# Prompt attention: the two maps of a differential head joined into one P row

## The chip, the cores and the metric

The kernel runs on one core of one Trainium2 chip. The metric is the device time of one execution in microseconds. Matmuls run on TensorE (PE; its weight loads are PEld), row arithmetic on VectorE (DVE), exponentials and copies out of PSUM on ScalarE (ACT); GpSimd (POOL) and the DMA queues are the others. Engines run their own instruction lists in order and meet only at semaphores.

## The reference, cut to what matters

One layer of a hybrid encoder over a prompt of 2048 tokens with 16 leading meta tokens (2064 rows), and over eight sampled streams. The stage in question is attention over the prompt:

```python
# group A: 8 heads of 64; each query attends to its top 256 admissible keys
_, sel = lax.top_k(score, k_top)
p = jax.nn.softmax(logits, axis=-1)
o = einsum('bqhk,bqkd->bqhd', p, v_sel)
# group B: 4 differential heads, two maps c each, values of 128
logits = einsum('bqhcd,blhcd->bhcql', qb, kb) * DH_B ** -0.5
logits = where(adm, logits - slope * dist, -inf)
p = softmax(logits, axis=-1)
a = p[:, :, 0] - lam * p[:, :, 1]
o = einsum('bhql,blhe->bqhe', a, vb)
```

After it come an RMS norm over each head of B, the output projection and an MLP.

## The kernel before, in words

The kernel is five stages with a barrier after each: keys' projection, queries' projection with the index scores, attention of the samples, attention of the prompt (`attend_prompt`), and the feed-forward stage. Only `attend_prompt` matters here.

It walks over 16 tiles `t` of 128 queries. Tile `t` sees `n = 16 + 128 (t + 1)` keys. In each tile there are 16 jobs `g % JOBS = m`: m = 0 to 7 are the heads of A, m = 8 to 15 are the eight maps of B, two by two. One job is, in order:

- PE: the logits of 128 queries by `n` keys, in pieces ("halves") of 1024 columns into one of two buffers `LG` (line 1098). They are computed two jobs ahead, inside the apply of an earlier job.
- VectorE, `take` (line 1270): adds the distances (`DT`, or `DA` for heads of A, where the keys that are not selected are far away), writes the row `X`, and keeps the maximum `mx`; line 1276 multiplies the maximum by the slope (`nm`).
- ScalarE, `softmax` (line 1179): the exponential in place, with its sum `sm`.
- PE, `apply`: transposes of `X` in groups of four 128-blocks into two banks `TP` (line 1125), ScalarE's copy of each group to `PTr` (line 1202), products of `PTr` with the values into `PV` (line 1138).
- VectorE: reciprocal of the sum (line 1284), and the output: line 1303 for A; for B line 1306 puts the first map's result into `OM`, and line 1311 adds the second's, multiplied by minus lambda over its sum (`rl`, line 1291).

There are two rows `X`, so the mask pass of job g + 1 waits for the transposes of job g - 1 (`s_tr`).

Beside the jobs VectorE finds for tile t + 1 each query's 256th largest index score: 25 halvings, each a count over the row. VectorE counts every other one (line 825, between the small steps 830 and 834), ScalarE the rest by signs (line 1187, `count_signs`). Nine last steps (lines 838 to 854, one of them a scan, line 846) make the row `DA`. The function `select_steps(m)` gives the steps of each job: halvings in jobs 2 to 14, the last steps in jobs 14 and 15, in front of the mask pass of the next tile's first job.

At a tile's end `finish` takes the norms of the four B heads, GpSimd raises them to the power -0.5 (lines 1066 and 1069), `finish_scale` applies them, and PE and ScalarE transpose the tile's output at job 2 of the next tile. SyncE's queue loads keys, values, queries and scores and stores the transposed output.

## Time and profile before

| | |
|---|---|
| median of 3 runs | 4177.35 us (4172.96 to 4182.59) |
| the profiled execution | 4171.43 us, span 4169.9 us |
| PE busy, whole span | 3748.4 us (90%) |
| VectorE busy | 2326.8 us (56%) |
| ScalarE busy | 1676.0 us (40%) |
| GpSimd busy | 186.8 us (4%) |
| prompt attention | about 995 to 2376 us of the span |
| PE, VectorE, ScalarE busy in it | 1181, 1068, 920 us |
| granted TensorE clock in it | 0.92 of full speed |

How to read it: an engine's busy time is a sum over the whole stage, but the tiles differ: early ones are short and full of small instructions, late ones long and full of matrix work, and the last has no selection beside it. So the stage is read tile by tile and job by job. The chain of work that ended last lies wholly in the feed-forward stage, behind the barrier, and says nothing about this stage.

### The profile page before, as it was taken

Reading aid. Unit: us, or ns where it says so; the run is one execution under the profiler, and the core shown is the slowest. Engines: PE = TensorE matmul, PEld = TensorE weight load, DVE = VectorE, ACT = ScalarE, POOL = GpSimd, SP = SyncE. Lnnn points to the kernel's source line nnn. Section 1 sums busy time; section 2 is a strip of 40 time slices with the busy share of each in tenths; the row PEclk is TensorE's granted clock in tenths of the full one; section 3 lists DMA queues with packets and bytes.
Section 4 is the critical chain, followed back from the end, with each engine's and each line's share of the span. In section 5 each row is a group of like instructions: output and inputs, shape, how many; then the busy total and the mean of one; then the engine's idle time right before and its main releaser. Section 6 shows DMA issues by size and latency. Waiting matters only on the chain. (4 is left out here: it accounts for less than half of the span.)

```text
span 4169.9 us, 56226 instructions
## 1 busy us (share of the span) xinstructions
PE 3748.4 (90%) x20713; PEld 3178.6 (76%) x20713; DVE 2326.8 (56%) x4784; ACT 1676.0 (40%) x2562; POOL 186.8 (4%) x373
## 2 busy tenths in 40 slices
PE   8989996884788988888988799999999999989997
PEld 6877883443677878888987678877888788779996
DVE  4335651444788888888775344445445444544334
ACT  2223431112566767777875422232323232322221
POOL 0001110000000000000000010001000100010000
PEclk9999995996799999999999899999999999999998
DMA  5556435627322121111100132223223322322121
GB/s 156 156 153 207 158 131 170 201 69 194 74 50 55 40 51 35 35 36 37 26 16 16 52 131 86 105 101 131 101 101 111 111 102 99 126 96 80 61 79 46
DMA packets 279876, 394.51 MB, mean 95 GB/s; under 512 B 29584, under 2 KB 181136, under 8 KB 270864
## 3 DMA queue, kind: packets, MB, share of 16 engines
q1 hardware_dynamic: 244208, 336.77, 25.9%
q0 software_dynamic: 12160, 44.18, 3.3%
q10 hardware_dynamic: 23328, 11.22, 1.1%
q8 instruction: 106, 1.74, 0.2%
q14 instruction: 74, 0.61, 0.0%
HBM read 320.32 MB, written 71.80 MB: 94 GB/s over the span
## 5 line engine op out<-in xcount | busy, mean ns | idle before, releaser
L1138 PE MATMUL pPV<-pV,pPTr 128*128 128x128 f32 (+1 forms) x4864 | 651.4, 282 | 36.8 <-ACT pPTr L1202 21.4
L1138 PEld LDWEIGHTS pPV<-pV,pPTr 128*128 128x128 f32 x4864 | 613.8, 198 | 57.6 <-issue 15.7
L1202 ACT ACTIVATE pPTr<-pTP 128x512 f32<-128x512 f32 (+3 forms) x704 | 355.7, 535 | 284.2 <-PE pTP L1125 281.5
L2167 ACT ACTIVATE fRU<-fUP 128x512 f32<-128x512 f32 (+1 forms) x128 | 80.0, 625 | 930.6 <-PE fUP L2037 930.6
L2037 PE MATMUL fUP<-fA_hi,fW_hi 128*128 128x512 f32 (+1 forms) x1280 | 418.9, 360 | 20.0 <-DVE fA_lo L2209 20.0
L2037 PE MATMUL fDN<-fW_hi,fU_hi 128*128 128x512 f32 x1088 | 423.6, 389 | 2.1 <-DVE fY L2307 2.1
L2037 PE MATMUL fDN<-fW_lo,fU_hi 128*128 128x512 f32 x1088 | 423.4, 389 | 0.0
L2037 PE MATMUL fDN<-fW_hi,fU_lo 128*128 128x512 f32 x1088 | 423.2, 389 | 0.0
L2037 PE MATMUL fUP<-fA_lo,fW_hi 128*128 128x512 f32 (+1 forms) x1280 | 418.3, 359 | 0.0
L2037 PE MATMUL fUP<-fA_hi,fW_lo 128*128 128x512 f32 (+1 forms) x1280 | 417.8, 359 | 0.0
L2203 DVE TENSOR_TENSOR fW_lo<-fW_raw,fW_hi 128x2048 fp32r<-128x2048 f32 x144 | 333.3, 2336 | 129.6 <-ACT fW_hi L2122 129.6
L1125 PE MATMUL pTP<-pidn,pX 128*128 128x128 f32 x2432 | 363.5, 281 | 35.0 <-ACT pX L1179 28.1
L1179 ACT ACTIVATE pX<-pX,pnm 128x144 f32<-128x144 f32 (+15 forms) x256 | 311.1, 1215 | 125.2 <-DVE pnm L1276 125.1
L2307 DVE TENSOR_TENSOR fY<-fDN,fY 128x512 f32<-128x512 f32 x272 | 183.6, 690 | 283.7 <-PE fDN L2037 283.7
L1125 PEld LDWEIGHTS pTP<-pidn,pX 128*128 128x128 f32 x2432 | 296.4, 152 | 39.7 <-ACT pX L1179 29.3
L1098 PE MATMUL pLG<-pK,pQA 128*128 128x512 f32 (+4 forms) x704 | 186.8, 399 | 138.2 <-DVE pmx L1270 103.5
L2122 ACT ACTIVATE fW_hi<-fW_raw 128x2048 fp32r<-128x2048 f32 x144 | 270.1, 1901 | 26.7 <-DMA fW_raw<-w_o 21.6
L2282 DVE TENSOR_TENSOR fU<-fRU 128x512 f32<-128x512 f32 (+1 forms) x128 | 92.9, 725 | 336.4 <-ACT fRU L2167 336.4
L2037 PEld LDWEIGHTS fUP<-fA_hi,fW_hi 128*128 128x128 f32 x1280 | 232.0, 189 | 51.8 <-issue 21.1
L1098 PEld LDWEIGHTS pLG<-pK,pQA 128*128 128x128 f32 x704 | 136.5, 212 | 165.8 <-DVE pmx L1270 92.5
L825 DVE TENSOR_SCALAR_CACHE_REDUCE pjunk<-pS,psv 128x272 int8<-128x272 f32 (+14 forms) x180 | 257.3, 1430 | 6.4
L2037 PEld LDWEIGHTS fUP<-fA_hi,fW_lo 128*128 128x128 f32 x1280 | 231.7, 189 | 30.6
(237 smaller groups left out, 6254.2 us busy)
## 6 DMA issues: line engine op xcount, KB each, us to landing
fW_raw<-w_up SPq DMA_DIRECT2D x64, 1024.0 KB, 5.0
fW_raw<-w_down SPq DMA_DIRECT2D x64, 1024.0 KB, 4.9
qT<-qOUT SPq DMA_DIRECT2D x40, 512.0 KB, 3.3
sKB<-cache_kb SPq DMA_DIRECT2D x8, 2048.0 KB, 14.0
sVB<-cache_vb SPq DMA_DIRECT2D x8, 2048.0 KB, 8.4
pQA<-qT SPq DMA_DIRECT2D x64, 256.0 KB, 4.9
pQB<-qT SPq DMA_DIRECT2D x64, 256.0 KB, 5.0
fW_raw<-w_o SPq DMA_DIRECT2D x16, 1024.0 KB, 5.5
```

The source lines that it names most:

```text
L825: ins = dve.tensor_scalar(junk, S, mid, 0.0, ALU.is_ge, ALU.add, accum_out=cnt)
L1098: mm = pe.matmul(dst[:, b - a:b - a + size], q[:, u, :], K[:, km, b:b + size], start=(u == 0), stop=(u == 1))
L1125: tr = pe.transpose(bank[:, j - 4 * k, :], X[g % 2][:, j * P:(j + 1) * P], idn[:, :])
L1138: mm = pe.matmul(PV[g % 2][:, 0:size], PTr[n % 3][:, j - 4 * k, :], V[:, j, a:a + size], start=(j == 0), stop=(j == blk[t] - 1))
L1179: act.activation(X[g % 2][:, 0:n_of[t]], X[g % 2][:, 0:n_of[t]], ACT.Exp, bias=nm[:, g % 2:g % 2 + 1], scale=slope, accum_out=sm[:, g % 2: ...
L1202: act.activation(PTr[n % 3][:, 0:size, :], TP[bank_use[("p", n)] % 2][:, 0:size, :], ACT.Copy).then_inc(s_pt, 1)
L2037: mm = pe.matmul(o, stationary[a], m[b], start=first and i == 0, stop=last and i == 2)
L2122: act.activation(W_hi[j // 2][:, (j % 2) * 2048:(j % 2) * 2048 + 2048], W_raw[j % 2][:, :], ACT.Copy).then_inc(s_whi, 1)
L2167: act.activation(RU[:, 0:nt * P].rearrange("p (n w) -> p n w", n=n), UP[f % 2][:, 0:n, 0:width], ACT.Relu).then_inc(s_ru, 1)
L2203: dve.tensor_tensor(W_lo[j // 2][:, col], W_raw[j % 2][:, :], W_hi[j // 2][:, col].bitcast(F32), ALU.subtract).then_inc(s_wlo, 1)
L2282: dve.tensor_tensor(U2[:, 0:nt * P], RU[:, 0:nt * P], RU[:, 0:nt * P], ALU.mult).then_inc(s_u2, 1)
L2307: dve.tensor_tensor(Y[:, t, cols], DN[o % 4][:, :], Y[:, t, cols], ALU.add)\
```

## The change

For a differential head with unnormalised rows e1, e2 and sums s1, s2 the result is (e1/s1 - lam e2/s2) V. The new kernel forms the row e1 + c e2 with c = -lam s1/s2, transposes and multiplies that one row, and scales the output by 1/s1.

- `applied(g)`: only the odd maps of B have an apply. An even map's place in PE's order holds its logits-ahead alone.
- `combine` on VectorE: the coefficient `cf`, then one pass over the first three quarters of the columns (`cut(t)`). GpSimd joins the last quarter in two passes, a product and a sum. The apply waits for both (`s_cb`, `s_pa`).
- There are three rows `X` (`XB`), and logits, mask pass and exponential run one job further ahead (`AHEAD = 3`; `take(g + 2)`, `softmax(g + 2)`).
- The mask pass takes the slope itself (scale `-SLOPE[m]`, minimum in place of maximum), and `nm` with its instruction goes.
- Reciprocals are taken for two jobs at once (`invert_sums`), at even jobs; `OM` and `rl` leave the outputs.
- Inside an apply only the first piece of the coming logits stands early, the others before the last group of products (before: the first two early).
- The selection starts and ends a job earlier: sign counts in jobs 0 to 12, the nine last steps in job 13. It stands last in VectorE's job, and no longer has outputs and reciprocals between its small steps.
- `lam4` lies in `OT`.

```diff
+    XB, AHEAD = 3, 3
+    def applied(g):
+        return g % JOBS < H_A or g % 2 == 1
...
-        X = [sb(f"X{i}", [P, XW]) for i in range(2)]
+        X = [sb(f"X{i}", [P, XW]) for i in range(XB)]
...
+        def cut(t):
+            return n_of[t] // 32 * 24
...
         def counted_by_sign(m):
-            return 2 * (m - 1) if 0 <= 2 * (m - 1) < HALVINGS else None
+            return 2 * m if 2 * m < HALVINGS else None
         def select_steps(m):
+            last = HALVINGS // 2
             if m == 0:
+                return 0, 1
+            if m <= last:
+                return count(2 * m - 2) + 1, count(2 * m)
+            if m == last + 1:
+                return count(2 * m - 2) + 1, SEL
+            return SEL, SEL
...
+            def combine(g):                      # GpSimd
+                t = g // JOBS
+                j = combined_before(g)
+                part = slice(cut(t), n_of[t])
+                x = X[(g + 1) % XB][:, part]
+                c = cf[:, j % 2:j % 2 + 1].to_broadcast([P, n_of[t] - cut(t)])
+                pool.wait_ge(s_cf, j + 1)
+                pool.tensor_tensor(x, x, c, ALU.mult).then_inc(s_pm, 1)
+                pool.wait_ge(s_pm, j + 1)
+                pool.tensor_tensor(x, x, X[g % XB][:, part], ALU.add).then_inc(s_pa, 1)
...
             def apply(g):                        # PE
                 if m < H_A:
+                    pe.wait_ge(s_ex, g + 1)
                 else:
+                    pe.wait_ge(s_cb, combined_before(g))
+                    pe.wait_ge(s_pa, combined_before(g))
...
-                        queries_keys(g + 2, slice(0, 2))
+                        logits(g + AHEAD, slice(0, 1))
                     products(k - 1)
-                if g + 2 < NG:
-                    queries_keys(g + 2, slice(2, None) if early else slice(None))
+                if g + AHEAD < NG:
+                    logits(g + AHEAD, slice(1, None) if early else slice(None))
                 products(groups[t] - 1)
...
             for g in range(NG):
-                apply(g)
+                if applied(g):
+                    apply(g)
+                elif g + AHEAD < NG:
+                    logits(g + AHEAD)
...
+            def invert_sums(g):                  # VectorE
+                i = g % 4
+                dve.wait_ge(s_ex, g + 2)
+                if g >= 4:
+                    dve.wait_ge(s_out, outputs_before(g - 2))
+                dve.reciprocal(ri[:, i:i + 2], sm[:, i:i + 2]).then_inc(s_ri, 1)
+            def combine(g):
+                dve.wait_ge(s_ri, g // 2 + 1)
+                if j >= 2:
+                    dve.wait_ge(s_pm, j - 1)
+                dve.tensor_scalar(c, sm[:, i:i + 1], lv[:, 5:6], ri[:, i + 1:i + 2], ALU.mult, ALU.mult)\
+                    .then_inc(s_cf, 1)
+                dve.wait_ge(s_cf, j + 1)
+                x = X[(g + 1) % XB][:, 0:n]
+                dve.scalar_tensor_tensor(x, x, c, X[g % XB][:, 0:n], ALU.mult, ALU.add).then_inc(s_cb, 1)
...
             take(0)
+            take(1)
             for g in range(NG):
+                if g + 2 < NG:
+                    take(g + 2)
+                if m % 2 == 0:
+                    invert_sums(g)
+                    if m >= H_A:
+                        combine(g)
+                if g > 0 and applied(g - 1):
+                    output(g - 1)
                 if m == 0 and t > 0:
                     finish(t - 1)
+                if t + 1 < PT:
+                    for k in range(*select_steps(m)):
+                        select(t + 1, k)
                 if m == 0 and t > 0:
                     finish_scale(t - 1)
```

## Rows read from the trace of the kernel before

**Rows 1.** Windows: the stage, then tiles 3, 9, 13 and 15; busy us per engine.

```profile
995.00:2376.00 1381.00, 1181.38 (x8827) 1107.13 (x8828) 1068.04 (x3131) 920.23 (x1636) 19.24 (x32) 0.92 0.20 47
...
1153.00:1210.00 57.00, 46.42 (x315) 43.32 (x315) 47.12 (x183) 35.93 (x93) 1.49 (x4) 0.86 0.25 55
...
1569.00:1661.00 92.00, 81.09 (x634) 77.34 (x632) 78.68 (x215) 67.20 (x109) 1.31 (x3) 0.94 0.17 39
...
1987.00:2108.00 121.00, 107.92 (x857) 102.83 (x856) 97.49 (x215) 87.61 (x125) 1.20 (x2) 0.94 0.11 23
...
2241.00:2373.00 132.00, 122.24 (x949) 113.01 (x947) 50.92 (x146) 69.62 (x110) 1.23 (x3) 1.00 0.02 5
```

**Rows 2.** Waits inside the stage: total us, times, longest.

```profile
DVE pX L1270 <- PE pTP L1125: 163.4, 91, 6.0
...
PE pLG L1098 <- DVE pmx L1270: 107.1, 27, 14.9
```

**Rows 3.** Timeline of VectorE at the end of tile 13: start, us.

```profile
2079.53 2.23 DVE L840 TENSOR_SCALAR_CACHE_REDUCE pDA<-pS,psv 128x1936 f32<-128x1936 f32 x1
...
2096.60 1.22 DVE L1270 CUSTOM_DVE_ANT_0 pX<-pLG,pDA 128x1024 f32<-128x1024 f32 x1
```

**Rows 4.** Timeline of one job B of tile 13, PE and VectorE.

```profile
2056.29 1.22 DVE L1270 CUSTOM_DVE_ANT_0 pX<-pLG,pDT 128x1024 f32<-128x1024 f32 x1 [0.43 <-PE pTP L1125]
...
2058.45 1.88 PE L1098 MATMUL pLG<-pK,pQB 128*128 128x512 f32 x8
...
2058.75 0.15 DVE L1276 TENSOR_SCALAR pnm<-pmx 128x1 f32<-128x1 f32 x1
...
2059.38 2.23 DVE L825 TENSOR_SCALAR_CACHE_REDUCE pjunk<-pS,psv 128x1936 int8<-128x1936 f32 x1
...
2060.16 1.05 PE L1138 MATMUL pPV<-pV,pPTr 128*128 128x128 f32 x8
...
2062.91 1.23 DVE L1270 CUSTOM_DVE_ANT_0 pX<-pLG,pDT 128x1024 f32<-128x1024 f32 x1 [0.72 <-PE pTP L1125]
```

**Rows 5.** Costliest groups: ScalarE's copies of transposed blocks.

```profile
L1202 ACT ACTIVATE pPTr<-pTP 128x512 f32<-128x512 f32 (+3 forms) x704 | 355.7, 535 | 284.2 <-PE pTP L1125 281.5
```

**Rows 6.** VectorE passes with two row operands: ns min/median/max over the 15 tiles.

```profile
L844 DVE SCALAR_TENSOR_TENSOR pDA<-pS,psv,pDA x15: 502/1434/2369, 1035.7 to 2210.3; 128x272 f32<-128x272 f32 x1, 128x400 f32<-128x400 f32 x1, 128x528 f32<-128x528 f32 x1, 128x656 f32<-128x656 f32 x1
```

**Rows 7.** Feed-forward stage: GpSimd's add alone, then one among VectorE's subtracts.

```profile
2430.30 1.89 POOL L2011 TENSOR_TENSOR fY<-fconst 128x1024 f32<-128x1024 f32 x1 [28.24 <-ACT fY L2145]
...
2445.70 2.21 POOL L2011 TENSOR_TENSOR fY<-fconst 128x1024 f32<-128x1024 f32 x1 [13.51 <-ACT fY L2145]
...
L2203 DVE TENSOR_TENSOR fW_lo<-fW_raw,fW_hi x2: 2280/3131/3982, 2446.1 to 2450.0; 128x2048 fp32r<-128x2048 f32 x2
```

**Rows 8.** Timeline: outputs of jobs 7, 15 of tile 9; last copies, tile 13.

```profile
1607.65 0.28 DVE L1303 TENSOR_SCALAR pO<-pPV,pri 128x64 f32<-128x64 f32 x1
...
1659.12 0.35 DVE L1311 SCALAR_TENSOR_TENSOR pO<-pPV,prl,pOM 128x128 f32<-128x128 f32 x1
...
2036.45 0.49 ACT L1202 ACTIVATE pPTr<-pTP 128x384 f32<-128x384 f32 x1 [0.58 <-PE pTP L1125]
...
2103.93 0.49 ACT L1202 ACTIVATE pPTr<-pTP 128x384 f32<-128x384 f32 x1 [0.62 <-PE pTP L1125]
```

**Rows 9.** Timeline of VectorE in tile 15: the mask passes of two jobs B.

```profile
2339.02 1.22 DVE L1270 CUSTOM_DVE_ANT_0 pX<-pLG,pDT 128x1024 f32<-128x1024 f32 x1 [4.51 <-PE pTP L1125]
...
2347.56 1.23 DVE L1270 CUSTOM_DVE_ANT_0 pX<-pLG,pDT 128x1024 f32<-128x1024 f32 x1 [4.66 <-PE pTP L1125]
```

**Rows 10.** Windows of PE alone in tiles 1 and 2: busy, granted clock.

```profile
1061.00:1064.00 3.00, 2.76 (x12) 0.50 0.58 175
...
1098.00:1100.00 2.00, 0.00 (x0) 1.00 0.18 33
...
1102.00:1104.00 2.00, 2.00 (x11) 0.50 0.00 0
...
1110.00:1112.00 2.00, 1.89 (x12) 0.70 0.50 154
```

More of the change, by code:

```diff
@@ L869, in attend_prompt @@
     NG = PT * JOBS
+    SLOPE = SLOPE_A + [s for s in SLOPE_B for _ in range(2)]
+    def applied(g):
+        return g % JOBS < H_A or g % 2 == 1
     sems = []
@@ L944, in groups_before, with outputs_before, combined_before @@
         def groups_before(g):
-            return sum(groups[i // JOBS] for i in range(g))
+            return sum(groups[i // JOBS] for i in range(g) if applied(i))
+        def outputs_before(g):
+            return sum(1 for i in range(g) if applied(i))
+        def combined_before(g):
+            return sum(1 for i in range(g) if not applied(i))
         def bank_users():
-            logits, banks, use_of, bank_use = [], [], {}, {}
-            def logit(kind, n, free):
-                use_of[kind, n] = len(logits)
-                logits.append(free)
+            banks, bank_use = [], {}
             def bank(kind, n, free):
@@ L1063, in _ @@
             pool.wait_ge(s_half, 1)
-            for t in range(PT):
-                pool.wait_ge(s_fq, 4 * (t + 1))
-                pool.tensor_scalar(fs[:, 4:8], fs[:, 0:4], 1.0 / DV_B, EPS, ALU.mult, ALU.add)\
-                    .then_inc(s_fe, 1)
-                pool.wait_ge(s_fe, t + 1)
-                pool.tensor_tensor(fs[:, 4:8], fs[:, 4:8], half[:, :], ALU.pow).then_inc(s_fr, 1)
+            def combine(g):
[8 more added lines that the diff above has]
+                pool.tensor_tensor(x, x, X[g % XB][:, part], ALU.add).then_inc(s_pa, 1)
+            for t in range(PT + 1):
+                if t > 0:
+                    pool.wait_ge(s_fq, 4 * t)
+                    pool.tensor_scalar(fs[:, 4:8], fs[:, 0:4], 1.0 / DV_B, EPS, ALU.mult, ALU.add)\
+                        .then_inc(s_fe, 1)
+                    pool.wait_ge(s_fe, t)
+                    pool.tensor_tensor(fs[:, 4:8], fs[:, 4:8], half[:, :], ALU.pow).then_inc(s_fr, 1)
+                if t < PT:
+                    for m in range(H_A, JOBS, 2):
+                        combine(t * JOBS + m)
         @block.tensor
@@ L1089, in free_bank, with logits @@
                 return TP[u % 2]
[L1091 to L1102 removed]
+            def logits(g, some=slice(None)):
                 t, m = divmod(g, JOBS)
@@ L1162, in finish @@
                     tr.then_inc(s_ft, 1)
-            queries_keys(0)
-            queries_keys(1)
+            for g in range(AHEAD):
+                logits(g)
             for g in range(NG):
@@ L1193, in take @@
                 t = g // JOBS
-                for k in range(groups[t]):
-                    if k == 2 and g + 1 < NG:
-                        softmax(g + 1)
+                for k in range(groups[t] if applied(g) else 0):
+                    if k == 2 and g + 2 < NG:
+                        softmax(g + 2)
                     n = groups_before(g) + k
@@ L1203, in take @@
                                    ACT.Copy).then_inc(s_pt, 1)
-                if groups[t] <= 2 and g + 1 < NG:
-                    softmax(g + 1)
+                if (groups[t] <= 2 or not applied(g)) and g + 2 < NG:
+                    softmax(g + 2)
             def finish(t):
@@ L1229, in _ @@
             dve.wait_ge(s_c, 80)
-            dve.memset(X[0][:, :], 0.0).then_inc(s_x0, 1)
-            dve.memset(X[1][:, :], 0.0).then_inc(s_x0, 1)
+            for i in range(XB):
+                dve.memset(X[i][:, :], 0.0).then_inc(s_x0, 1)
             for i in range(2):
@@ L1273, in take @@
                         .then_inc(s_lx, 1)
-                slope = (SLOPE_A + [s for s in SLOPE_B for _ in range(2)])[m]
-                dve.wait_ge(s_lx, halves_before(g + 1))
-                dve.tensor_scalar(nm[:, i:i + 1], mx[:, i, halves[t] - 1:halves[t]], -slope, None, ALU.mult)\
-                    .then_inc(s_nm, 1)
-            def invert_sum(g):
-                i = g % 2
-                dve.wait_ge(s_ex, g + 1)
-                if g > 0:
-                    dve.wait_ge(s_out, g)
-                dve.reciprocal(ri[:, i:i + 1], sm[:, i:i + 1]).then_inc(s_ri, 1)
```

202 lines of the change are left out of this document (84 added, 118 removed).

## The prediction

> **What bounds the kernel now.** I read the windows over the stage first, then the waits inside it, then the timeline of single jobs. Prompt attention holds 1381 us of the 4169.9 us span [rows 1], and the profiled execution took 4171.43 us, 5.9 us under the median of 4177.35. Everything else is untouched and a barrier closes the stage, so whatever the stage gains or loses the kernel gains or loses. The windows look like a TensorE stage: PE is busy 1181 of the 1381 us [rows 1]. Over the tiles the picture changes. In tile 3 VectorE is busy 47 of 57 us and PE 46, in tile 9 it is 79 and 81 of 92, in tile 13 97 and 108 of 121, and in tile 15, which has no selection left to do, 51 and 122 of 132 [rows 1]. The short gaps between VectorE's instructions, 183 to 215 in these tiles, come on top, so it is nearly full in every tile up to 9 and not far from it in 13.
>
> The waits say when each sets the pace. VectorE waits 163 us for transposes (it is ahead, PE sets the pace) and PE waits 107 us for VectorE's mask pass pmx [rows 2]. Nearly all of these 107 us are one gap at each tile's end: in tile 13 the last selection passes run from 2079.53 to the mask pass at 2096.60, and PE stands still for most of these 17.1 us [rows 2, 3]. The reader is to see that a tile's second half, where heads B lie, is where VectorE is already worst off.
>
> One job of tile 13 (n = 1808 keys) in the timeline [rows 4]: the period from mask pass to mask pass is 6.62 us, 0.72 us of it VectorE's wait for PE. So VectorE needs 5.9 us: two mask pieces and their accumulators until the small ones begin, 2.45 us (2056.29 to 2058.75); count pass 2.23; the rest small instructions. PE needs all 6.62: logits 1.71 (2058.45 to 2060.16), and the apply (transposes and products) the other 4.9.
>
> **What the change removes.** Four of sixteen applies per tile. From tile 13, 4.9 us for 15 blocks is 0.33 us a block; over all tiles 4 x 152 blocks give 200 us of PE work. ScalarE loses a quarter of the 356 us of P copies [rows 5], about 80. On VectorE go 256 maximum-times-slope instructions pnm (0.15 us each [rows 4], of which I count the 0.1 that the next does not overlap, 25 us), one 0.35 us output per head, and the small lambda product.
>
> **What it adds.** Per head B a VectorE pass over three quarters of the row with two row operands. The same kind of instruction takes 0.50 us at 272 elements and 2.37 at 2064 [rows 6]: 0.22 + n/960. At 0.75 n that is 0.63 us in tile 3, 1.23 in tile 9, 1.63 in tile 13, 1.83 in tile 15; over the 64 heads about 71 us. The coefficient before it takes 0.3 with its wait (a one-column product took 0.15 [rows 4], the wait as much), and the reciprocal, today inside the gap between two dependent small steps of the selection, now costs its own 0.2 per pair. Today's interleaving of small steps with outputs goes too (0.1 a job). Sum over the stage: +71 +19 +25 for the additions, -25 -22 -6 for the removals, +20 for lost interleaving: some 80 us more on VectorE against 200 less on PE.
>
> GpSimd makes two passes over n/4. Its nearest row is a two-operand add of 1024 elements in 1.89 us [rows 7], so 0.9 us for 464 elements in tile 13, 1.9 for both. It starts together with VectorE's pass. The rows show what happens when both want two operands from SBUF: an add that met VectorE's subtracts took 2.21 us, and the subtract that began at 2446.1, inside it, 3.98 against 2.28 for the next [rows 7]: 1.7 longer, the add's remainder. They took turns. I take it that they do here: VectorE goes first (its own wait is shorter than one across engines), GpSimd then needs 1.9 us more, so the joined row is ready 3.5 us after the coefficient, not 2. If GpSimd went first at each pass, VectorE would lose 0.9 to 1.9 us a head in tile 13. The Trainium skill (SBUF — State Buffer, section SBUF: two separate sides) says that VectorE and GpSimd share one port pair as an exclusive lock, whose loser waits for the whole instruction; by that rule GpSimd's passes and VectorE's never overlap, and the trace agrees (3.98 against 2.28 us). Without it the joined row would be ready 1.5 us earlier.
>
> **The three P rows.** The next mask pass still waits for the transposes of the job before, as now; the exponential gets one job more of slack. VectorE's own work per job is what it was, so jobs of heads A should stay within 0.1 us. The third memset lies beside the stage's first loads of keys and queries; without that cover it is a copy of one row, 2 us once. Tile 0 as a whole is held by those loads and stays.
>
> **Heads B with selection, tile 13.** Even loop on VectorE: mask 2.42, reciprocal and coefficient 0.5, join 1.63, output 0.35, selection step 3.2, together 8.1. Odd loop: 2.42 + 3.2 = 5.6. Pair: 13.7 against 2 x 6.62 = 13.24 now. A wait comes on top: the second piece of the next logits now stands before the last products, and these wait for copies that ScalarE makes only after the exponential; I get 0.4 to 1 us per pair, 14.1 in all. The selection starts and ends one job earlier (last passes in job 13, not 14 and 15), which gives back what these three pairs lose. After the last passes, however, comes mask, coefficient, join, GpSimd, apply of job 15 in series: 9.7 us to its last transpose, against 7.3 now, plus 1.7 for taking turns. Tile 13: 67.2 us for the eight B jobs against 67.5 now (last copy of job 7 to last copy of job 15, 2036.45 to 2103.93 [rows 8]), +1.7 for the turns.
> The same sum for others. Tile 9: pairs of 11.3 + 0.4, the B half 53.9 (turns included) against 51.5 now (outputs at 1607.65 and 1659.12 [rows 8]), +2.4. Tile 3, all VectorE: the added 0.7 us in each of four heads has no cover, +2.7. Tiles 11 and 12 0 to -1, tile 14 -4, where PE's 16 blocks weigh more, each +1.7 for turns. I take +2.2 for each of tiles 1 to 10 (+22) and 0 for the four of 11 to 14 together (-5 and +6).
>
> **Tile 15.** A job takes 8.54 us now (2339.02 to 2347.56), a pair 17.1, VectorE waiting 4.5 in each job [rows 9]. PE's part falls to 5.6 + 4.2 = 9.8. But the row's mask, coefficient, join and GpSimd (3.0 + 0.5 + 1.8 + 2.1), first piece of the next mask 1.3, and transposes up to the last 5.8 form one chain: 14.9 with turns, 13.1 without. Four pairs: -9 (or -16). The A jobs gain 0.5 us each, since the third piece of logits no longer waits for a mask: -4. Together -13.
>
> **Further costs.** (1) GpSimd's two passes run on beside VectorE's selection steps, of which one (0.21 us, two operands) can meet them: 0 to 1 us in each of 45 pairs; I take 0.3, +14. (2) The clock. In tile 2 PE stands still from 1098 to 1100 (and a little on both sides), the granted clock goes from 1.00 to 0.50 (2.4 to 1.2 GHz), and PE is full until it rises in 1110 to 1112; in tile 1 it is at 0.50 with PE 2.76 of 3 us busy [rows 10]. In the new B pairs PE works 8.3 of 14 us (tile 13) or 3.4 of 6.8 (tile 3), with a gap of up to 3.9 us in each. At half clock the apply of tile 13 is 9.8 us and the pair some 18. From 0 (no fall) to 4 us on 50 pairs (200); as most of the doubled work lies in VectorE's shadow I take 0.3 us a pair, +15.
> Sum: +22 +0 -13 +14 +15 = +38: 4209 for the profiled execution, 4215 by the median; I say 4210.
>
> **Rivals.**
> A. PE's relief counts (faster). PE's time per tile falls from 108 to 88 us in tile 13, and if the three rows let VectorE run through the tile without waiting, tile 13 would take its 97 busy us, 7 for the joins and a few between instructions, about 108 instead of 121. For it: the 163 us of waits [rows 2]. Against it: those waits lie in heads A, which stay PE-paced, and the join falls where VectorE is full. Half of it would give 7 us on tiles 11 to 14 and 3 on 7 to 10: -40, with tile 15 at -20 and +10 on tiles 1 to 6: 4171 - 50 = 4121. It decides if, in tile 13, a B pair takes under 12.5 us. Milder: turns cost nothing and the clock holds, 4171 + 38 - 14 - 15 - 20 = 4160.
> B. No change: the sum without (1) and (2), 4171 + 9 = 4180.
> C. The clock stays at half through the B jobs: 2 to 3 us a pair, +100 to 150 in place of 15: 4300.
> D. GpSimd takes the port first: VectorE loses 0.3 to 1.9 us a head, mean 0.8, +51 in place of 14: 4245.
>
> **Numbers.** The forecast's case (4185 to 4235) 0.38, A with its milder form 0.22, B 0.14, C 0.08, D 0.18. The range leaves out most of C and the lower half of A: 4145 to 4265. A measurement tells 0.2% (8 us) from no change. Faster 0.23, same 0.15, slower 0.62.
>
> **What would show it.** Products and transposes each at three quarters of their count or less; VectorE busy in the stage near 1060 (by their own durations 84 us come and 94 go, but what goes lay partly in others' gaps); the B pair of tile 13 near 14 us and of tile 9 near 11.7; join passes of 1.6 us and GpSimd passes of 0.9 beginning where the join ends; PE's gap at the end of tile 13 between 12 and 14 us; a granted clock under 0.9 in the B jobs. The prediction is wrong if B pairs take less time than two jobs do now while selection runs, or if tile 15 gains much over 15 us.

## The result and the profile after

The changed kernel takes 4242.8 us (median, 4233.8 to 4258.2) against 4177.7 in the same comparison: ratio 1.016, interval 1.0134 to 1.0185. It is 65 us slower where I forecast 33 us more. Its profiled span is 4232.2 us. One execution of e9 below took 7250.9 us, far outside all the others, and is left out of that kernel's median.

Windows of the changed kernel: the stage, then tiles 3, 9, 13 and 15 (span, then busy us of PE, PEld, DVE, ACT and POOL, granted clock, DMA share, GB/s), to be laid beside [rows 1].

```profile
995.00:2438.00 1443.00, 1088.12 (x6992) 992.72 (x6993) 1130.15 (x2739) 838.03 (x1455) 154.22 (x160) 0.82 0.19 44
1159.00:1217.00 58.00, 42.23 (x252) 39.08 (x251) 48.01 (x157) 32.80 (x83) 5.29 (x10) 0.79 0.24 54
1605.00:1704.00 99.00, 75.18 (x498) 68.92 (x497) 83.80 (x189) 60.88 (x97) 10.74 (x9) 0.84 0.15 36
2048.00:2177.00 129.00, 100.01 (x678) 92.33 (x677) 106.19 (x190) 80.01 (x109) 14.46 (x10) 0.84 0.10 21
2316.00:2435.00 119.00, 100.00 (x725) 90.75 (x724) 53.81 (x117) 56.84 (x88) 15.88 (x9) 0.96 0.02 5
```

The reader is to see three things. Tiles 9 and 13 lose 7 and 8 us, and tile 15 gains 13. PE loses only 93 us of busy time where I reckoned 200 us of applies gone: what was left ran longer, at a granted clock of 0.82 in the stage where it was 0.92. VectorE is busy 1130 us, 62 more, where I forecast slightly less than before.

Groups of the changed kernel in the stage (count | busy us, mean ns | idle before), VectorE's join, GpSimd's add, VectorE's small selection step, GpSimd's product:

```profile
L1330 DVE SCALAR_TENSOR_TENSOR pX<-pX,pcf 128x96 f32<-128x96 f32 (+15 forms) x64 | 100.7, 1573 | 2.3
L1082 POOL TENSOR_TENSOR pX<-pX 128x48 f32<-128x48 f32 (+15 forms) x64 | 92.2, 1441 | 5.0
L834 DVE SCALAR_TENSOR_TENSOR psv<-psv,pwidths 128x1 f32<-128x1 f32 x360 | 86.6, 241 | 12.8
...
L1080 POOL TENSOR_TENSOR pX<-pX,pcf 128x48 f32<-128x48 f32 (+15 forms) x64 | 42.7, 667 | 1162.0 <-DVE pcf L1326 1162.0
```

The joins sum to 100.7 us, not the 71 reckoned (by the formula that I used, over the 64 rows of 70.7 thousand columns in all, three quarters are in truth 69). The small step sums to 86.6 us; the same 360 are 79.1 in e3 below, where GpSimd joins nothing.

Waits of the changed kernel inside the stage (total us, times, longest), beside [rows 2]:

```profile
ACT pjunk L1216 <- DVE psv L834: 168.9, 93, 4.9
PE pLG L1123 <- DVE pmx L1304: 160.5, 44, 13.3
...
DVE pX L1304 <- PE pTP L1145: 122.6, 65, 6.1
...
PE pTP L1145 <- DVE pX L1330: 86.9, 40, 9.8
```

TensorE waits 160 us for mask passes (107 before) and 87 for joins. ScalarE's sign pass waits 169 us for the selection's small step, 41 before.

One B pair of tile 13 in the timeline of the changed kernel (start, us), beside [rows 4]:

```profile
2097.09 1.23 DVE L1304 CUSTOM_DVE_ANT_0 pX<-pLG,pDT 128x1024 f32<-128x1024 f32 x1 [0.61 <-PE pTP L1145]
...
2099.85 0.27 DVE L1326 TENSOR_SCALAR pcf<-psm,plv,pri 128x1 f32<-128x1 f32 x1
2100.16 2.42 DVE L1330 SCALAR_TENSOR_TENSOR pX<-pX,pcf 128x1344 f32<-128x1344 f32 x1
2100.21 0.96 POOL L1080 TENSOR_TENSOR pX<-pX,pcf 128x464 f32<-128x464 f32 x1 [50.67 <-DVE pcf L1326]
2101.25 2.35 POOL L1082 TENSOR_TENSOR pX<-pX 128x464 f32<-128x464 f32 x1
...
2102.87 0.74 DVE L834 SCALAR_TENSOR_TENSOR psv<-psv,pwidths 128x1 f32<-128x1 f32 x1
...
2103.70 1.06 PE L1145 MATMUL pTP<-pidn,pX 128*128 128x128 f32 x8 [2.73 <-issue]
...
2106.26 1.23 DVE L1304 CUSTOM_DVE_ANT_0 pX<-pLG,pDT 128x1024 f32<-128x1024 f32 x1
2106.37 1.91 ACT L1216 ACTIVATE pjunk<-pS,psv 128x1936 int8<-128x1936 f32 x1 [4.69 <-DVE psv L834]
...
2107.55 2.07 PE L1123 MATMUL pLG<-pK,pQB 128*128 128x512 f32 x4 [2.79 <-DVE pmx L1304]
...
2108.28 1.06 ACT L1231 ACTIVATE pPTr<-pTP 128x512 f32<-128x512 f32 x2
...
2109.42 1.91 PE L1158 MATMUL pPV<-pV,pPTr 128*128 128x128 f32 x8
...
2113.54 1.23 DVE L1304 CUSTOM_DVE_ANT_0 pX<-pLG,pDT 128x1024 f32<-128x1024 f32 x1 [1.82 <-PE pTP L1145]
```

The pair takes 16.45 us; two jobs took 13.24, and I forecast 14.1. The even loop (2097.09 to 2106.26) takes 9.17 us, 8.1 forecast; the odd one 7.28, 5.6 forecast. GpSimd's product runs its 0.96 us at once and VectorE's join beside it takes 2.42. GpSimd's add, 1.17 us in e5 below, takes 2.35 and ends 1.02 us after the join's end at 2102.58, so it seems to have waited for the join. VectorE's one-column step, 0.22 us elsewhere, takes 0.74 and ends with the add. TensorE stands twice, 2.73 and 2.79 us, and works behind the second stand at half its rate: four logits matmuls take 2.07 us, where [rows 4] have eight in 1.88, and eight products 1.91, where they have 1.05. The next mask pass waits 1.82 us for transposes that lie behind them. Windows of TensorE alone in this pair (busy us, granted clock), during the first stand, the second, and after it:

```profile
2101.00:2103.00 2.00, 0.00 (x0) 1.00 0.00 0
...
2105.00:2107.00 2.00, 0.00 (x0) 0.61 0.00 0
...
2109.00:2111.00 2.00, 2.00 (x10) 0.50 0.04 8
```

The clock is full (2.4 GHz) through the first stand and the eight transposes after it, falls in the second, and is half (1.2 GHz) while TensorE is busy without a break behind it.

### The profile page after: what moved, and what is told of

Read it like the earlier page. It is cut to its first block and busy times, and to the rows that moved or that the text cites. A ratio compares the mean times of both kernels' runs of the same rounds, so it can differ in the third digit from the quotient of the medians.

```text
span 4232.2 us, 51929 instructions
## 1 busy us (share of the span) xinstructions
PE 3656.6 (86%) x18889; PEld 3066.2 (72%) x18889; DVE 2392.5 (57%) x4401; ACT 1595.1 (38%) x2386; POOL 320.9 (8%) x501
## 5 line engine op out<-in xcount | busy, mean ns | idle before, releaser
L1158 PE MATMUL pPV<-pV,pPTr 128*128 128x64 f32 (+1 forms) x3648 | 547.6, 299 | 41.2 <-ACT pPTr L1231 33.1
L1158 PEld LDWEIGHTS pPV<-pV,pPTr 128*128 128x128 f32 x3648 | 529.0, 218 | 69.3 <-issue 48.5
L1145 PE MATMUL pTP<-pidn,pX 128*128 128x128 f32 x1824 | 300.9, 301 | 131.1 <-DVE pX L1330 86.9
L1206 ACT ACTIVATE pX<-pX,pmx 128x144 f32<-128x144 f32 (+15 forms) x256 | 310.3, 1212 | 187.3 <-DVE pmx L1304 186.7
L1231 ACT ACTIVATE pPTr<-pTP 128x512 f32<-128x512 f32 (+3 forms) x528 | 267.5, 535 | 237.9 <-PE pTP L1145 234.1
L1123 PE MATMUL pLG<-pK,pQA 128*128 128x512 f32 (+4 forms) x704 | 220.3, 438 | 146.0 <-DVE pmx L1304 109.7
L1145 PEld LDWEIGHTS pTP<-pidn,pX 128*128 128x128 f32 x1824 | 239.7, 163 | 146.8 <-DVE pX L1330 96.1
L1216 ACT ACTIVATE pjunk<-pS,psv 128x272 int8<-128x272 f32 (+14 forms) x180 | 227.7, 1265 | 169.2 <-DVE psv L834 168.9
L1123 PEld LDWEIGHTS pLG<-pK,pQA 128*128 128x128 f32 x704 | 145.5, 232 | 172.3 <-DVE pmx L1304 96.0
```

What stands on the lines that cost most here:

```text
L1123: mm = pe.matmul(LG[:, h % 2, b - k * L:b - k * L + size], q[:, u, :], K[:, km, b:b + size], start=(u == 0), stop=(u == 1))
L1145: tr = pe.transpose(bank[:, j - 4 * k, :], X[g % XB][:, j * P:(j + 1) * P], idn[:, :])
L1158: mm = pe.matmul(pv[:, 0:size], PTr[n % 3][:, j - 4 * k, :], V[:, j, a:a + size], start=(j == 0), stop=(j == blk[t] - 1))
L1206: act.activation(X[g % XB][:, 0:n_of[t]], X[g % XB][:, 0:n_of[t]], ACT.Exp, bias=mx[:, g % 4, k:k + 1], scale=-1.0, accum_out=sm[:, g % 4: ...
L1216: act.activation(junk[:, 0:n], S[t % 2][:, 0:n], ACT.Sign, bias=sv[:, 2:3] if h else 0.0, scale=-1.0, accum_out=sv[:, 3:4]).then_inc(s_sel, 1)
L1231: act.activation(PTr[n % 3][:, 0:size, :], TP[bank_use[("p", n)] % 2][:, 0:size, :], ACT.Copy).then_inc(s_pt, 1)
```

## The experiments

Times are medians, ratios are to the kernel before on the same chip, where that took 4175.6 to 4178.4 us. "A tile's time" is the distance of GpSimd's norm steps in the profiled execution, a "pair" half of the distance from job 10's first mask pass to job 14's. Since the changed kernel's mask passes run two jobs ahead, these are VectorE's loops over jobs 8 to 11.

**The parts of the change.** e1: no head is joined, all else of the change stays; e2: joined in tile 15 alone.

```diff
+    def joined(t): return False        # e2: t == PT - 1
-        return g % JOBS < H_A or g % 2 == 1
+        return g % JOBS < H_A or g % 2 == 1 or not joined(g // JOBS)
```

> No head is joined: both maps of B are transposed and multiplied as before, with the second output's lambda product. Kept are the three P rows, the work one job further ahead, the slope inside the mask pass, paired reciprocals and the earlier selection. If the loss comes from the join itself (its pass, the turns with GpSimd, a PE that stands still and falls to half clock), this is within 10 us of the kernel before, 4177. Rival, the restructuring costs by itself (the long chain after the last selection passes, the later second piece of logits): 4195 to 4215. The A half of tile 13, 53.4 us before and 56.0 after, tells the same: 53.5 by the first, 56 by the second.

Measured: 4150.3 us, ratio 0.9936 (0.9919 to 0.9953), outside what I expected. The rest of the change is worth 28 us by itself. Of the 19 us by which the profiled spans differ, 9 lie in tile 15 (132.0 to 122.9 us), which has no selection.

> Heads are joined in tile 15 alone, where no selection runs; the other tiles are as in the kernel that joins none. Tile 15 took 12.5 us less in the changed kernel while every tile with selection took more. If that gain belongs to the tile, this is 10 to 14 us under the kernel that joins none, so about 4165, under the kernel before. Rival, the gain came only from a late start that the tiles before it caused: within 4 us of the kernel that joins none.

Measured: 4148.5 us, ratio 0.9925 (0.9909 to 0.9942). Tile 15 takes 119.6 us: with GpSimd's quarter the join itself brings only 3 us there. The whole is 2 us under e1 where 10 to 14 were expected. That is the rival's number, but not its cause: most of tile 15's gain is there without any join.

e3: VectorE joins all columns. e4: it joins 32 of them, and nobody the rest.

```diff
         def cut(t):
-            return n_of[t] // 32 * 24
+            return n_of[t]                 # e4: 32
...
-                    pe.wait_ge(s_pa, combined_before(g))
```

> VectorE joins all columns, GpSimd none. By the port theory (the two engines take turns, 30 us on the join passes and 10 on a small selection step) VectorE's join passes sum to 64 x 0.22 + 70.7K elements / 960 = 88 us instead of 101 and the small step L834 is back at 0.21 us; the joined row is ready 1.2 us earlier in tile 13. Time 4243 - 22 to - 40, so 4203 to 4221, with a pair of heads in tile 13 about 1.5 us shorter. Rival, GpSimd's quarter is real help for a VectorE that sets the pace: 18 us more, 4255 to 4265.

Measured: 4196.1 us, ratio 1.0046 (1.0032 to 1.006), 7 us under the range of the port theory; the rival fell. GpSimd's quarter, meant as help, costs 47 us. The joins and the small step in this kernel:

```profile
L1327 DVE SCALAR_TENSOR_TENSOR pX<-pX,pcf 128x144 f32<-128x144 f32 (+15 forms) x64 | 87.6, 1369 | 2.3
L834 DVE SCALAR_TENSOR_TENSOR psv<-psv,pwidths 128x1 f32<-128x1 f32 x360 | 79.1, 220 | 12.8
```

VectorE needs 87.6 us for the whole rows and 100.7 for three quarters of them when GpSimd takes the rest.

> Left out of the computation: the join of all but the first 32 columns (the even map counts nowhere else), and GpSimd's passes. What is left is PE's relief with coefficient and one short pass. It bounds what the apply's removal is worth. By the theory that VectorE's join work and the turns are the loss: the 101 us of join passes fall to 16 and 10 us more with them, so 4243 - 70 to - 95, 4150 to 4175, a few us under the kernel before at best. Rival, the clock and the chain at the tiles' ends set the pace: 4200 to 4230, with the granted clock in B jobs still at half.

Measured: 4124.4 us, ratio 0.9869 (0.9852 to 0.9885), 26 us under the expected range; the rival fell. The kernel leaves most of the join out, so it is a bound and no version to use. Its short joins:

```profile
L1327 DVE SCALAR_TENSOR_TENSOR pX<-pX,pcf 128x32 f32<-128x32 f32 x64 | 16.1, 252 | 2.3
```

Without its pass the join is worth 26 us against e1; the pass over the whole row on VectorE alone costs the 72 us between e4 and e3, for 87.6 - 16.1 = 71.5 us of VectorE's work. That the two agree so closely is partly chance: over tiles 1 to 15 of the profiled executions e3 is 58 us longer than e4. In tile 13, where four joins of 0.25 us became 2.10, the tile takes 7.3 us more for 7.4 us of work, so there little or nothing covers it. The relief of TensorE lies where TensorE is the bound: against e1, e4 gains 18 us in tile 15 (122.9 to 105.1) and 2 us in tiles 1 to 14 together, where the granted clock is lower too (0.86 against 0.93 over tiles 1 to 15).

e8: the kernel before, with the slope in the mask pass.

```diff
-                                             scale=1.0, scalar=mx[:, i, k - 1:k] if k else -3.0e38,
-                                             op0=ALU.add, op1=ALU.max, accum_out=mx[:, i, k:k + 1])\
+                                             scale=-SLOPE[m], scalar=mx[:, i, k - 1:k] if k else 3.0e38,
+                                             op0=ALU.add, op1=ALU.min, accum_out=mx[:, i, k:k + 1])\
...
-                dve.tensor_scalar(nm[:, i:i + 1], mx[:, i, halves[t] - 1:halves[t]], -slope, None, ALU.mult)\
...
-                               bias=nm[:, g % 2:g % 2 + 1], scale=slope,
+                               bias=mx[:, g % 2, halves[t] - 1:halves[t]], scale=-1.0,
```

> The kernel before with one part of the change: the slope goes into the mask pass (as minus the slope, with a running minimum), so that the 256 one-column instructions maximum times slope go and the exponential waits for the mask pass itself. Theory 1 (this is what made the kernel without any join 28 us faster than before): 15 to 28 us less than 4178, so 4150 to 4163. Rival (the gain comes from the third row and from logits three jobs ahead, most of it in tile 15, and the small instruction was hidden): 4170 to 4180 us, with tile 15 still at 130 us or more.

Measured: 4168.5 us, ratio 0.9985 (0.9974 to 0.9997): 7 of the 28 us, with an interval that nearly reaches no change. That is 1.5 us under the rival's range, and tile 15 takes 132.2 us, as the rival says. The other 21 us the third row, the deeper logits, the order of their pieces, the paired reciprocals and the earlier selection share; these weren't taken apart.

**The order at the port.** e5: VectorE's join first.

```diff
                 pool.wait_ge(s_cf, j + 1)
+                pool.wait_ge(s_cb, j + 1)
                 pool.tensor_tensor(x, x, c, ALU.mult).then_inc(s_pm, 1)
```

> The changed kernel, but GpSimd's product also waits for VectorE's join, so that VectorE has the port first. Theory 1 (the order at the port costs VectorE its time): the join of tile 13 falls from 2.42 us to 1.6 to 1.7, but GpSimd's two passes then lie wholly behind it, where they can hold up the selection's small two-operand step longer, and the joined row is ready no earlier (1.6 + 1.0 + 1.0 = 3.6 us after the coefficient). Half of the 0.8 us a head stays: 4205 to 4230 us. Rival (it is the moment at which the joined row is ready, not VectorE's time, that sets the pair): the joins get shorter and the time does not, 4235 to 4255 us.

Measured: 4238.0 us, ratio 1.0142 (1.012 to 1.0164), an interval that overlaps the changed kernel's: the rival holds. The same place of tile 13, then the joins and the small step over the stage:

```profile
2096.36 1.62 DVE L1331 SCALAR_TENSOR_TENSOR pX<-pX,pcf 128x1344 f32<-128x1344 f32 x1
...
2098.12 0.96 POOL L1081 TENSOR_TENSOR pX<-pX,pcf 128x464 f32<-128x464 f32 x1 [52.38 <-DVE pX L1331]
2098.27 0.83 DVE L834 SCALAR_TENSOR_TENSOR psv<-psv,pwidths 128x1 f32<-128x1 f32 x1
...
2099.16 1.17 POOL L1083 TENSOR_TENSOR pX<-pX 128x464 f32<-128x464 f32 x1
...
L834 DVE SCALAR_TENSOR_TENSOR psv<-psv,pwidths 128x1 f32<-128x1 f32 x360 | 90.9, 252 | 12.7
L1331 DVE SCALAR_TENSOR_TENSOR pX<-pX,pcf 128x96 f32<-128x96 f32 (+15 forms) x64 | 68.4, 1069 | 2.3
```

The join is back at 1.62 us, as forecast, but the joined row is ready 3.97 us after the join's start, 3.44 in the changed kernel and 2.10 in e3, and the small step is held up longer. Together the two groups sum to 159.3 us of VectorE, 28 less than in the changed kernel and 7 less than in e3, and still the kernel is 42 us slower than e3. So the price of the quarter isn't VectorE's longer passes alone: it is also the row that is ready later. By the tiles, e5 gains 12 us in tiles 1 to 14 and loses 4 in tile 15, where VectorE isn't the bound. Which of the two engines goes first therefore matters little in the sum.

**Queues in a B pair.** e7: two pieces of the logits early.

```diff
-                        logits(g + AHEAD, slice(0, 1))
+                        logits(g + AHEAD, slice(0, 2))
```

> The changed kernel with the first two pieces of the logits three jobs ahead behind the second group of transposes, as the kernel before had it two jobs ahead, in place of the first piece alone. If VectorE's waits for the second piece (53 us in 74 waits) are on the path: 10 to 30 us less, 4213 to 4233. Rival: TensorE would now wait there for a free half of the logits bank before the products, and what VectorE gains goes back: 4235 to 4260 us.

Measured: 4260.3 us, ratio 1.0208 (1.0187 to 1.0228), 17 us more than the changed kernel and at the upper edge of the rival's range. The rival holds: over the stage TensorE now waits 168.5 us for mask passes ahead of its logits (160.5 in the changed kernel), and VectorE 155.7 us for transposes (122.6).

e9 and e10: ScalarE's sign pass of an even B job behind the first two P copies of the odd one.

```diff
                                    ACT.Copy).then_inc(s_pt, 1)
+                    if k == min(1, groups[t] - 1) and not applied(g - 1) and t + 1 < PT:
+                        h = counted_by_sign(g % JOBS - 1)
+                        if h is not None:
+                            count_signs(t + 1, h)
...
-                if t + 1 < PT and counted_by_sign(m) is not None:
+                if t + 1 < PT and counted_by_sign(m) is not None and applied(g):
```

> The changed kernel with ScalarE's sign pass of every even B job put behind the first two P copies of the odd job after it. New theory: in a B pair ScalarE reaches that sign pass while VectorE still joins; the pass waits for the selection's small step behind the join (4.69 us at 2106.37 in tile 13, 169 us in 93 waits over the stage, 41 in the kernel before), and the copies of the joined row, transposed at 2104.8, stand behind it until 2108.3. With the copies first, the products start some 3 us earlier in each pair of tile 13, VectorE's next mask pass finds its row free, and a pair takes 14 to 15 us in place of 16.6: 60 to 110 us less over some 45 pairs, 4135 to 4185. Rival (the pair is set by VectorE's own work and the joined row's readiness): at most 15 us less, since the selection then gets its count later: 4228 to 4250.

> The same move of the sign pass, with VectorE joining all columns and GpSimd none (4196 us without the move). New theory: also 40 to 90 us less, 4105 to 4155, the pair of tile 13 near 13.5; and GpSimd's quarter costs less than the 47 us that it cost with the sign pass in front, since part of what it cost was that wait made longer. Rival (VectorE's own work sets the pair): 4180 to 4196, and GpSimd's quarter costs the same 47.

Measured: 4245.0 us (ratio 1.0164, 1.0144 to 1.0185) and 4196.4 us (1.0052, 1.0035 to 1.0068). Nothing came of the 60 to 110 and 40 to 90 us: that theory fell. e10's timeline says why:

```profile
2077.99 1.09 PE L1143 MATMUL pTP<-pidn,pX 128*128 128x128 f32 x8 [1.35 <-DVE pX L1331]
...
2078.68 1.09 ACT L1229 ACTIVATE pPTr<-pTP 128x512 f32<-128x512 f32 x2 [1.34 <-PE pTP L1143]
...
2082.36 2.07 PE L1122 MATMUL pLG<-pK,pQB 128*128 128x512 f32 x4 [3.28 <-DVE pmx L1305]
...
2084.23 1.91 PE L1156 MATMUL pPV<-pV,pPTr 128*128 128x128 f32 x8
```

The copies are done at 2079.8, and the products still begin at 2084.2: the next logits stand ahead of them in TensorE's queue and wait for a mask pass. So e11 to e13 move those too.

```diff
-                early = g + AHEAD < NG and groups[t] > 1
+                early = g + AHEAD < NG and groups[t] > 1 and (m < H_A or t == PT - 1)
...
-                    if k == 2 and g + 2 < NG:
+                    if k == 2 and g + 2 < NG and not copies_first(g):   # e11, e12
```

> VectorE joins alone, and both in-order queues let the joined row through first: for the odd B jobs of tiles 0 to 14 TensorE takes the first piece of the later job's logits after the products instead of ahead of them, and ScalarE takes the P copies ahead of the exponential, with the sign pass of the job before behind the third copy. Theory 3 (the trace of the run with the sign pass later: transposes done at 2079.1 in tile 13, copies at 2079.8, products only at 2084.2, since TensorE stood 3.28 us at the logits for a mask pass that VectorE does only after join, output and selection): the products start right behind their copies, the apply is done before VectorE's next row but one, and the pair of tile 13 falls from 15.38 us to VectorE's own 13.7 to 14.3; 1 to 1.5 us on some 45 pairs, 4130 to 4160 us. Rival (a pair is VectorE's own work, waits included, whatever the queues do): 4185 to 4200.

> The same two moves in the changed kernel, GpSimd's quarter kept. Theory 3: the pair of tile 13 falls from 16.6 us to some 14.5 (GpSimd's passes still make the row ready 1.2 us later and hold up VectorE's join by 0.8), 4160 to 4200 us. Rival: 4230 to 4250.

> VectorE joins alone, and only TensorE's part of the move is made: the logits behind the products, ScalarE's order as in the changed kernel. If the two queues cover each other (either one alone holds the products): no more than 15 us less than 4196. If TensorE's queue alone held them: the whole 40 to 60 us.

Measured: 4203.8 (ratio 1.0063, 1.004 to 1.0086), 4275.7 (1.0239, 1.0218 to 1.026) and 4255.6 us (1.0187, 1.0166 to 1.0208). Theory 3 fell as well, and all three kernels are slower than the rivals had it. In e11 the pairs of tiles 11 to 14 do get shorter (15.01 in place of 15.38 us in tile 13), and these four tiles together take 5.9 us less than in e3. But in tiles 7 to 14 the loops over jobs 13 and 15, at the tile's end, get 1 to 3 us longer together, and tiles 1 to 10 take 22 us more. That the later logits are the reason is likely and not shown. Moving TensorE's part alone costs 59 us.

**The clock.** e6, e14, e15: useless products where TensorE stands. The edit shown is that of e15, which has them at both stands: behind the logits of the even job (the first stand; last lines of the edit) and inside the apply of the odd job (the second). e14 has the second alone, with `// 160` and VectorE joining alone; e6 the first alone, with `// P` and in all tiles.

```diff
+            def fill(g, times):                       # into the bank that the next products overwrite
+                ...
+                for _ in range(times if 1 < t < PT - 1 else 0):
+                    pe.matmul(PV[done % 2][:, 0:size], K[:, 1, 0:P], K[:, 1, 0:size], start=True, stop=True)
...
+                        if m >= H_A:
+                            fill(g - 1, n_of[t] // 256)
...
                     logits(g + AHEAD)
+                    fill(g, n_of[t] // 256)
```

> The changed kernel with useless TensorE products put behind the logits of every even B job, n/128 of them of up to 512 columns (14, some 3 us, in tile 13), written to the output bank that the next products overwrite, so that TensorE does not stand still while the row is joined. Theory 1 (the half clock in the B pairs costs time): the granted clock of tile 13's B jobs rises from 0.79 to 0.95 or more, the eight products of a group take 1.0 us again in place of 1.9, and a pair takes 1 to 2 us less: 4160 to 4200 us. Rival (VectorE sets the B pairs and the half clock lies in its shadow): the clock rises as well, and the time stays within 15 us of 4243 or grows by what of the 3 us is in the way.

> VectorE joins alone; in tiles 2 to 14 useless TensorE products (n/160 of up to 512 columns, 11 or some 2.4 us in tile 13) stand in each odd B job behind the second group of transposes, just where TensorE stands 3.28 us for the mask pass. Theory 4 (the half clock lies on the chain: in tile 13 logits 2.07 and products 1.91 at half speed come between VectorE's mask pass and the transposes for which its next mask pass waits 2.13): clock of the B jobs 0.95 or more, that wait mostly gone, the pair of tile 13 from 15.38 to 13.7 to 14.3, which is VectorE's own work; 4150 to 4175 us against 4196. Rival: the clock rises and the pair keeps within 0.3 us, 4190 to 4210.

> The changed kernel with such products at both places where TensorE stands in a B pair of tiles 2 to 14 (n/256 each, 7 in tile 13, 1.5 us each time), in place of n/128 at the first in all tiles (which gave 16 us back in tiles 1 to 13 and lost them again in 14 and 15, where they were in the way). Theory 4: clock 0.95 or more, the pair of tile 13 15.0 to 15.4 in place of 16.6, 4195 to 4220 us. Rival: within 10 us of 4243.

Measured: e6 4240.7 us (ratio 1.0159, 1.0137 to 1.0181): 15 us less in tiles 7 to 13, 4 more in tile 14, and pairs of 21.5 in place of 17.0 us in tile 15, where the added work stood in the way. The sum of e6 is thus the one that its rival named, though the gain in tiles 7 to 13 is the theory's. e14 4183.3 (1.002, 1.0007 to 1.0032), 13 less than e3; e15 4218.3 (1.0094, 1.0075 to 1.0114), 24 less than the changed kernel. Two pairs of tile 13 in each, windows of the changed kernel, of e15 and of e14 (columns as above):

```profile
2097.00:2130.00 33.00, 21.96 (x123) 19.65 (x122) 27.51 (x48) 19.25 (x24) 6.63 (x4) 0.79 0.00 1
```

```profile
2085.00:2115.00 30.00, 24.93 (x156) 20.59 (x155) 27.39 (x49) 19.17 (x25) 6.63 (x4) 1.00 0.00 1
```

```profile
2069.00:2097.00 28.00, 23.17 (x147) 19.35 (x147) 25.45 (x46) 18.79 (x25) 0.00 (x0) 1.00 0.00 1
```

The granted clock is 0.79 in the first and 1.00 in the others, and the same two pairs take 33, 30 and 28 us. The mask passes of e14's jobs 10 to 12 in tile 13:

```profile
2069.75 1.22 DVE L1313 CUSTOM_DVE_ANT_0 pX<-pLG,pDT 128x1024 f32<-128x1024 f32 x1 [0.61 <-PE pTP L1153]
...
2078.07 1.22 DVE L1313 CUSTOM_DVE_ANT_0 pX<-pLG,pDT 128x1024 f32<-128x1024 f32 x1
...
2083.64 1.23 DVE L1313 CUSTOM_DVE_ANT_0 pX<-pLG,pDT 128x1024 f32<-128x1024 f32 x1
```

The wait before the last has gone and the odd loop takes 5.57 us. Theory 4 holds for these pairs. Of the sum that I drew from it only part came (e14: 4183 where 4150 to 4175 was expected, e15 at the edge of what was), so the other loops of a tile gave next to nothing back. The trace of e14 shows where part of the gain went: in the last odd job of a tile. TensorE in it, then VectorE's mask pass of the next tile's job 2:

```profile
2133.07 2.84 PE L1134 MATMUL pPV<-pK 128*128 128x512 f32 x11
...
2135.75 1.09 PE L1122 MATMUL pLG<-pK,pQA 128*128 128x512 f32 x4
...
2139.42 1.23 DVE L1313 CUSTOM_DVE_ANT_0 pX<-pLG,pDA 128x1024 f32<-128x1024 f32 x1 [5.31 <-PE pTP L1153]
```

The eleven useless products take 2.84 us in front of work for which that mask pass waits. From job 1's mask pass of tile 14 to job 2's it is 7.86 us, 5.37 in e3. Over tiles 7 to 13 this loop takes 13 us more than in e3, against 18 us less in the four loops of the two pairs that were measured.

| tile | pair: after | e3 | e15 | e14 | two jobs, e1 |
|---|---|---|---|---|---|
| 7 | 11.56 | 10.15 | 9.79 | 9.48 | 8.34 |
| 9 | 12.98 | 12.17 | 11.30 | 10.82 | 9.65 |
| 11 | 15.28 | 14.63 | 13.27 | 12.64 | 11.86 |
| 13 | 16.60 | 15.38 | 14.80 | 13.99 | 13.24 |

**The better version.** e16 is e2 with VectorE joining alone.

> The changed kernel with the join in tile 15 alone, made by VectorE over all columns; GpSimd joins nothing, and in tiles 0 to 14 both maps are applied. Tile 15 took 115.7 us with VectorE alone, 119.6 with GpSimd's quarter and 122.9 without a join, so by tiles 1 to 14 of the run without any join (4150): 4141 to 4147 us, the fastest whole kernel of the study. Rival (the difference in tile 15 came from the tiles before it): 4148 to 4152.

Measured: 4139.5 us, ratio 0.991 (0.9896 to 0.9924), 1.5 us under the expected range and the fastest kernel of the study that leaves nothing out. Two of its mask passes in tile 15, two jobs apart, beside [rows 9], and the window between:

```profile
2307.51 1.23 DVE L1306 CUSTOM_DVE_ANT_0 pX<-pLG,pDT 128x1024 f32<-128x1024 f32 x1 [4.56 <-PE pTP L1148]
...
2321.58 1.23 DVE L1306 CUSTOM_DVE_ANT_0 pX<-pLG,pDT 128x1024 f32<-128x1024 f32 x1 [4.55 <-PE pTP L1148]
```

```profile
2293.00:2321.00 28.00, 21.03 (x144) 18.13 (x143) 16.78 (x32) 13.25 (x19) 0.00 (x0) 1.00 0.00 1
```

A pair takes 14.07 us, 17.1 before; here PE had 4.5 us a job of work left when VectorE was done, so an apply less is time less. Tile 15 takes 111.8 us, 122.9 in e1; that difference is the whole gain over e1 (4150.3 to 4139.5).

## Why the prediction came out as it did

**Direction and bound.** Slower was right, and the reason given is part of it: VectorE is full where the join falls, and e3 less e4 shows it (58 to 72 us for 71.5 us of pass). What I left out of the reason is that the row's lateness and the half clock lengthen the pairs as well.

**The sum.** By the runs, 4178 - 28 (e1) - 26 (applies gone, e4 less e1) + 72 (VectorE's pass, e3 less e4) + 47 (GpSimd's quarter) = 4243. By the distance of the norm steps over tiles 1 to 15 in the profiled executions the same four steps are -19, -20, +58 and +46, together the same 65. The forecast's +38 became +65, and these terms were mis-sized:

- *Port, "+14", with 1.7 a tile for turns.* This is the step that failed most. I reckoned GpSimd's quarter as relief for VectorE (71 us of joins) and one small collision of 0.3 us a pair. By my own numbers it was to cost some 21 us net: 14, and 1.7 in each of 14 tiles, less 17 for the quarter that VectorE needn't join. The quarter costs 47 us, 35 with TensorE kept busy (e15 less e14). It lengthens the joins by 100.7 - 68.4 = 32 us (68.4 is their group's sum in e5) and the small step by 7.5: in tile 13 0.80 and 0.52 us a pair, 1.3 in place of 0.3. The row is ready 1.3 us later than in e3, and e5 shows that this costs too.
- *Order at the port.* "VectorE goes first" was wrong in the changed kernel. GpSimd's product was served at once in the trace, and VectorE lost 32/64 = 0.5 us a head on the mean, where rival D has 0.8. D, priced at 4245, thus met the time, and its condition held. But turning the order round (e5) gives back only some 5 us, within the uncertainty, since the row is then later still; and the new order's -28 stands in no rival. The agreement of D's number is partly chance.
- *Clock, "0.3 us a pair, +15".* In tiles 7 to 13 the half clock costs 1.3 to 2.0 us in each of the two pairs measured (after less e15), 24 us or more in all; more, since the useless products themselves can stand in the way. The prediction took the doubled work to lie in VectorE's shadow. In the odd loop it doesn't: logits, products and transposes between two mask passes became 1.8 us of wait. "0.4 to 1 us of wait per pair" was too much at full clock (none in e14's odd loop) and too little at half. Rival C, the half clock all through, had 2 to 3 us a pair; the granted clock was 0.7 to 0.8 over the pairs of tiles 7 to 13.
- *Three rows and reordered small work, "0", and -4 for tile 15's A jobs.* Measured -28. The A jobs of tile 15 fell from 8.63 to 8.19 us as forecast (-3.5); that two maps applied in turn would gain 1 us a pair there too (17.09 to 16.13) I had not seen. This error hid part of the others.
- *Tiles 11 to 14, "0".* Measured +25.6 together; tiles 1 to 10 +52, where 22 and some 20 of the +29 for port and clock were reckoned. VectorE's own sum was nearly right: even loop 8.1 for three quarters of the row (e14, with the whole row: 8.32), odd loop 5.6 (5.57). That e14's pair, 13.99, lies beside the 14.1 is in part chance, since it has a longer join and no wait. What was missing lies in the terms for port and clock.
- *Tile 15, "-13".* Measured -12.6, and the agreement is luck: 9 of it come without any join (e1). The pairs stayed at 17.04 us in place of 14.9 (whose own terms add to 14.5), at a granted clock of 0.90. In e16, without GpSimd and at full clock, they take 14.07.

**Signs named ahead.** Products and transposes at three quarters of their count: yes. B pairs near 14 and 11.7 us: no, 16.6 and 13.0. VectorE busy near 1060: no, 1130, of which 40 us are the port. GpSimd's passes beginning where the join ends: no, the product began with it. Joined row ready 3.5 us after the coefficient: yes (2100.12 to 2103.60). Join passes of 1.6 us: only in e5. PE's gap at the end of tile 13 between 12 and 14: 11.2, after last passes that end at the same distance as in [rows 3]:

```profile
2159.49 1.22 DVE L1304 CUSTOM_DVE_ANT_0 pX<-pLG,pDA 128x1024 f32<-128x1024 f32 x1
...
2160.78 2.93 PE L1123 MATMUL pLG<-pK,pQA 128*128 128x512 f32 x6 [11.20 <-DVE pmx L1304]
```

Clock under 0.9 in B jobs: yes, 0.79. A jobs unchanged: 6.75 against 6.68 us in tile 13 (mean from job 2's mask pass to job 8's). Rival A would have had B pairs under 12.5 us in tile 13; even e4, with hardly a join, has 13.05.

**Open.** How the 21 us of the rest of e1 divide; how much of the quarter's 47 us is VectorE's time and how much the later row; what full clock would be worth with no useless product in the way; whether the third row or the order of the selection would matter more in tiles 2 to 6, where e14 still loses 27 us to e1.

## What to carry to other kernels

Before a piece of a pass is given to a second engine, ask whether both read through the same port: a quarter given away here made VectorE's own three quarters longer (100.7 us) than the whole (87.6), and the row was ready later. Work taken from an engine that isn't the bound brings next to nothing (2 us in tiles 1 to 14, e4 against e1, and 18 in tile 15), and where it leaves gaps in TensorE's work it can take the clock with it: reckon at half rate what then lies between two of the bound's instructions. Use such a change only where the profile has the bound on the other side, as in tile 15.

## What the runs showed of the hardware

- GpSimd's product and VectorE's join were recorded as starting within 0.05 us in the pair shown (0.04 to 0.12 us in all 64), VectorE's first, and it was VectorE's that was longer: 2.42 us against 1.62 alone, GpSimd's 0.96 in both cases. The Trainium skill (SBUF — State Buffer, section SBUF: two separate sides) gives the port to whichever starts first; by the recorded starts that is not what happened here, though the turns themselves nearly agree (VectorE lost 0.80 us beside a product of 0.96).
- A step on one column with two SBUF operands took 0.74 and 0.83 us in place of 0.22 beside a GpSimd pass, and ended with it: its size is no protection.
- With two stands of 2.7 and 2.8 us, only eight transposes between them, the granted clock was 0.79 over the pairs of tile 13: 1.00 in the first stand, 0.61 at the end of the second, 0.50 after it. With seven useless matmuls at each stand, 1.5 us, it was 1.00 (2.4 GHz), and the kernel was 24 us faster.
- Moving one in-order queue out of the way (e9, e10) gave nothing while another stood behind it, and moving both (e11) shortened the late tiles by 5.9 us together and lengthened tiles 1 to 10 by 22.
